# A final norm that moves into the experts' program, with the last expert's rows added by a one-hot product

## The chip, the cores and the metric

The kernel runs on one core of a Trainium2 chip. The metric is the device time of one execution in microseconds (us), smaller is better. The core has five engines that run their own instruction streams and meet at semaphores: TensorE (PE in the rows; PEld is its weight loading), VectorE (DVE), ScalarE (ACT), GpSimd (POOL) and SyncE (SP), which here only issues DMAs.

## What is computed

One encoder layer over a prompt of 512 and a sample of 1024 tokens of width 1024 (12 tiles of 128 tokens: 4 of the prompt, 8 of the sample). Attention and a state-space mixer come first; they are not touched. Then comes the mixture of experts, in which each of 16 experts chooses its tokens (64 of the prompt, 128 of the sample), and a last norm:

```python
def _ec_moe(h, w_router, w_gate, w_up, w_down):
    ...
    gate, idx = lax.top_k(aff.T, cap)
    xe = tok[idx]
    hid = jax.nn.silu(jnp.einsum('ecd,edf->ecf', xe, w_gate)) * jnp.einsum('ecd,edf->ecf', xe, w_up)
    ye = jnp.einsum('ecf,efd->ecd', hid, w_down) * gate[..., None].astype(h.dtype)
    out = jnp.zeros_like(tok).at[idx.reshape(-1)].add(ye.reshape(-1, d))
    return out.reshape(b, s, d)

    # in the layer, and after it
    return x + g2 * _ec_moe(h, w_router, w_gate, w_up, w_down)
    ...
    return _rmsnorm(x, final_norm_w)
```

All is in float32. The expert width is 2048.

## The kernel before

`encoder_layer` runs its stages one after the other. Each stage is a block of programs, one for each engine, and a barrier of all engines stands between blocks. The last two stages are `experts` and `final`.

`experts` walks through the 16 experts, and in each through 4 slabs (`fs`) of 512 hidden columns. A slab has 12 units of 128x1024 weights: for each of 4 column groups (`fc`) one of the gate (kind 0) and one of the up matrix (kind 1), then 4 of the down matrix (kind 2). A step is one `fc` of one `fs`, so an expert has 16 steps. SP loads the slabs in halves into three raw tiles (`raw[0]` and `raw[1]` lie in the tile `keys_or_w_out`, `raw[2]` is `slab_down`). ScalarE copies a unit to its high part (L2464), ten units ahead of TensorE; VectorE subtracts for its low part (L2524), eight units ahead. TensorE multiplies high and low parts (L2665, L2666), ScalarE and VectorE add the two halves up, take silu and product, and split the hidden values in two again (L2582 to L2587), and TensorE adds the down product to the banks `y_banks` (L2678, and L2642 for the prompt's low weights). TensorE begins step s only when the hidden values of step s-2 are there. The order on each engine is written out by hand in `body`. In steps 8 to 13 of every expert but the last, TensorE turns the next expert's gathered rows (`turn_x`) in spare columns of the banks, and ScalarE and VectorE drain them (`drain_x`).

When an expert is done, `weigh` on VectorE multiplies its rows by the gates and by a row of the layer's gate (L2563). The prompt's 64 rows lie in two halves of the bank, so ScalarE first copies one half (`copy_low`, L2480) and VectorE adds the other (L2560). POOL then scatters the 128 and the 64 weighted rows with an adding indirect DMA into the tensor `residual` in HBM (L2437). For all experts but the last this runs beside the next expert. For the last nothing runs beside it: POOL waits until both scatters have landed, and the block ends.

`final` is the next block. SP loads tile after tile of `residual` (L2735) into four buffers. ScalarE squares and sums (L2752) and takes the root (L2754), VectorE takes the reciprocal (L2768) and multiplies with it and the norm's weight (L2773), and POOL issues the store (L2743). The weight is first spread over the partitions by 8 small fp32 matmuls (L2001); the profile records an fp32 matmul that isn't a transpose as two. The first four tiles are the prompt's; the eight of the sample are a hardware loop of two turns. A load of a later tile waits for the product of the tile four before it.

## Time and profile before

| | us |
|---|---|
| median of three runs | 2969.93 |
| lowest and highest | 2969.90 and 2974.16 |
| the profiled execution, in all | 2971.95 |
| its span in the trace | 2970.3 |

The profile is of one execution. Times in the rows count from the start of its span. A timeline row gives start, length, engine, source line, operation, what is written and read, and in brackets the idle time ahead of it with what ended it. Rows with "x4" are merged: the length is that of all four from the first start to the last end. TensorE runs at 1.2 or 2.4 GHz; the granted clock of a stretch is 0.50 or 1.00 for these, and between them where it changed within the stretch.

### The profile page before, as it was taken

How to read it: one execution, taken by the hardware profiler on the slowest of the kernel's cores; microseconds unless marked ns; L12 is line 12 of the kernel's file. 1: busy time of each engine (PE TensorE's matmuls, PEld its weight loads, DVE VectorE, ACT ScalarE, POOL GpSimd, SP SyncE). 2: the span in 40 equal slices, each digit the busy share in tenths (PEclk: the TensorE clock that was granted, in tenths of full speed). 3: DMA queues.
4: the chain of work that ended last, by engine and by line, in shares of the span. 5: the costliest groups of instructions: out<-in, count | busy, mean ns of one | idle time of the engine just before them, and what ended most of it. 6: DMA issues, size and time to landing. Idle time of an engine off the chain costs nothing. (4 is left out here: it accounts for less than half of the span.)

```text
span 2970.3 us, 50523 instructions
## 1 busy us (share of the span) xinstructions
PE 2744.9 (92%) x17710; PEld 2391.8 (81%) x17710; DVE 2155.6 (73%) x4142; ACT 1522.5 (51%) x2876; POOL 219.5 (7%) x202
## 2 busy tenths in 40 slices
PE   5999687999988939999999999999999999999992
PEld 4999455566667738999999999999999999999992
DVE  3565776676765577878878878878878878778773
ACT  4453444444543315555555555555555555555552
POOL 0000022121110000000000000000000000000001
PEclk8999898999999969999999999999999999999996
DMA  6111310212224428678677677677677677677655
GB/s 258 67 64 58 121 39 30 96 59 95 100 89 155 155 106 275 219 243 257 221 242 254 223 239 254 220 241 254 222 241 253 222 244 250 223 247 249 223 182 181
DMA packets 359719, 547.39 MB, mean 184 GB/s; under 512 B 14785, under 2 KB 287937, under 8 KB 359617
## 3 DMA queue, kind: packets, MB, share of 16 engines
q1 hardware_dynamic: 350720, 514.59, 50.7%
q0 software_dynamic: 8896, 31.46, 4.6%
q8 instruction: 62, 1.02, 0.1%
q14 instruction: 41, 0.33, 0.0%
HBM read 493.51 MB, written 52.49 MB: 184 GB/s over the span
## 5 line engine op out<-in xcount | busy, mean ns | idle before, releaser
L2665 PE MATMUL banks<-rowsT_parts,weights_high 128*128 128x384 f32 x4096 | 1213.3, 359 | 11.6 <-DVE hidden_parts L2587 7.5
L2666 PE MATMUL banks<-rowsT_parts,weights_low 128*128 128x192 f32 x4096 | 1026.8, 251 | 0.0
L2666 PEld LDWEIGHTS banks<-rowsT_parts,weights_low 128*128 128x128 f32 x4096 | 781.8, 191 | 22.4
L2665 PEld LDWEIGHTS banks<-rowsT_parts,weights_high 128*128 128x128 f32 x4096 | 770.5, 188 | 23.3 <-DVE hidden_parts L2587 10.2
L2524 DVE TENSOR_TENSOR weights_low<-keys_or_w_out,weights_high 128x1024 fp32r<-128x1024 f32 x512 | 603.7, 1219 | 1.4 <-ACT weights_high L2464 1.4
L2464 ACT ACTIVATE weights_high<-keys_or_w_out 128x1024 fp32r<-128x1024 f32 x512 | 524.3, 1050 | 39.6 <-PEq L2262 39.6
L2574 DVE TENSOR_TENSOR h_or_keys_or_sums<-banks,h_or_keys_or_sums 128x192 f32<-128x192 f32 x512 | 181.8, 355 | 317.7 <-ACT h_or_keys_or_sums L2490 317.7
L2678 PE MATMUL banks<-weights_high,hidden_parts 128*128 128x512 f32 x1536 | 403.6, 391 | 0.0
L2490 ACT ACTIVATE h_or_keys_or_sums<-banks 128x192 f32<-128x192 f32 x512 | 165.6, 323 | 454.0 <-PE banks L2642 332.4
L2678 PEld LDWEIGHTS banks<-weights_high,hidden_parts 128*128 128x128 f32 x1536 | 283.5, 188 | 56.1
L2524 DVE TENSOR_TENSOR weights_low<-slab_down,weights_high 128x1024 fp32r<-128x1024 f32 x256 | 311.7, 1218 | 0.0
L2464 ACT ACTIVATE weights_high<-slab_down 128x1024 fp32r<-128x1024 f32 x256 | 262.6, 1051 | 0.0
L2498 ACT ACTIVATE silu_gate<-h_or_keys_or_sums 128x192 f32<-128x192 f32 x256 | 92.8, 363 | 228.0 <-DVE h_or_keys_or_sums L2574 228.0
L2642 PE MATMUL banks<-weights_low,hidden_parts 128*64 128x512 f32 x512 | 200.7, 393 | 0.0
L2437 POOL DMA_INDIRECT residual<-weighted,rows_out x32 | 49.8, 1555 | 1665.9 <-DVE weighted L2563 1665.9
L1825 PE MATMUL banks<-keys_or_w_out,arena_attend 96*128 96x512 f32 x320 | 160.8, 609 | 6.2 <-DVE arena_attend L1748 4.3
L2678 PE MATMUL banks<-weights_low,hidden_parts 128*128 128x512 f32 x512 | 157.7, 389 | 0.0
L1553 ACT ACTIVATE arena_attend<-banks 128x512 f32<-128x512 f32 (+1 forms) x96 | 50.5, 526 | 170.3 <-PE banks L1838 170.0
L2205 PE MATMUL banks<-w_out_high,mixed_parts 128*128 128x512 f32 x384 | 127.3, 399 | 2.8 <-DVE mixed_parts L2168 2.3
L1603 DVE TENSOR_REDUCE mix_top<-banks 128x1 f32<-128x1024 f32 (+1 forms) x96 | 100.2, 1043 | 25.4 <-PE banks L1825 25.4
L1838 PEld LDWEIGHTS banks<-masks,arena_attend 128*128 128x128 f32 x640 | 74.8, 141 | 53.4 <-issue 29.6
L995 PE MATMUL banks<-w_in_high,h_parts 128*128 128x512 f32 (+1 forms) x384 | 116.7, 381 | 0.0
(314 smaller groups left out, 3627.5 us busy)
## 6 DMA issues: line engine op xcount, KB each, us to landing
keys_or_w_out<-w_gate SPq DMA_DIRECT2D x128, 1024.0 KB, 5.3
keys_or_w_out<-w_up SPq DMA_DIRECT2D x128, 1024.0 KB, 6.9
slab_down<-w_down SPq DMA_DIRECT2D x128, 1024.0 KB, 4.9
arena_attend<-w_ada SPq DMA_DIRECT2D x8, 2048.0 KB, 7.6
arena_attend<-ssd_tiles SPq DMA_DIRECT2D x12, 992.0 KB, 9.1
arena_inputs<-w_ada SPq DMA_DIRECT2D x4, 2048.0 KB, 11.5
ssd_tiles<-arena_inputs SPq DMA_DIRECT2D x24, 256.0 KB, 2.0
mixed<-arena_attend SPq DMA_DIRECT2D x12, 512.0 KB, 2.9
```

Of the source, the lines that this page charges most:

```text
L995: mm = nc.tensor.matmul(out, a, b, start=(k == 0 and n == 0), stop=(k == KD - 1 and n == 2))
L1603: nc.vector.tensor_reduce(top[:, h % 2:h % 2 + 1], core.banks[:, h % 2 * 1024:h % 2 * 1024 + keys_n], AX_X, ALU.max).then_inc(topped, 1)
L1825: mm = nc.tensor.matmul(core.banks[:, h % 2 * 1024 + k0:h % 2 * 1024 + k0 + 512], qT[j][0:DQK, h, :], kT[0:DQK, h, k0:k0 + 512], start=Tru ...
L2205: mm = nc.tensor.matmul(core.ps[6 * j + half], a, b[:, k, cols], start=(k + n == 0), stop=(k == 7 and n == 2))
L2464: nc.scalar.activation(like(n, w_hi), unit_of(raw, n), ACT.Copy).then_inc(unit_hi, 1)
L2490: nc.scalar.activation(sums[:, kind, fc % 2], core.ps[2 * (fc % 2) + kind][:, CT:2 * CT], ACT.Copy).then_inc(low_out, 1)
L2524: nc.vector.tensor_tensor(like(n, w_lo), unit_of(raw, n), like(n, w_hi[:].bitcast(F32)), ALU.subtract).then_inc(unit_lo, 1)
L2574: nc.vector.tensor_tensor(sums[:, kind, fc % 2], core.ps[2 * (fc % 2) + kind][:, 0:CT], sums[:, kind, fc % 2], ALU.add).then_inc(sum_done, 1)
L2642: return nc.tensor.matmul(y_banks[1][0:CAP[0], cols], h_parts[:, fc, prompt_hi], w_lo[:, UNITS.index((2, fc)), cols], start=False, stop=en ...
L2665: nc.tensor.matmul(out[:, 0:2 * CT], w_hi[:, u, block], x[:, k, :], start=k == 0, stop=False)
L2666: mm = nc.tensor.matmul(out[:, 0:CT], w_lo[:, u, block], x[:, k, 0:CT], start=False, stop=k == KD - 1)
L2678: mm = nc.tensor.matmul(y_banks[b][:, cols], h_parts[:, fc, tokens], w[:, u, cols], start=step == 0 and first, stop=step == STEPS - 1 and ...
```

## The change

The stage `final` is gone; its work is done at the end of the block of `experts`.

- SP loads the residual's 12 tiles in three DMAs of four tiles into the three raw tiles, each when VectorE has read the last of the weights there, and once the scatters of the first 15 experts have landed. The tiles are taken in the order sample 0 to 7, prompt 0 to 3 (`tail`). The last expert's rows are not scattered.
- In steps 8 to 13 of the last expert, where the others turn and drain rows, TensorE spreads the final norm's weight and a row of numbers 0 to 127 (`tail_row`), and VectorE copies these, builds small columns (`slots`: each row's token number less the tile's first, and the prompt's gates, doubled over both halves of the partitions) and compares them into one-hot matrices, one of 128x128 for each tile (`tail_rows`). They lie in the buffers of the gathered rows, which now have 128 partitions for the prompt too.
- The prompt's rows are not added up before the weighing: all 128 partitions of the bank, both halves, are weighed at once, and the one-hot matrix has each token twice.
- TensorE multiplies for each tile the one-hot matrix with the weighted rows in fp32, two matmuls of 512 columns, in three pairs of banks in turn (`add_rows`). VectorE adds the bank to the loaded residual in place (`add_last`). ScalarE squares, sums and takes the root (`square`). VectorE takes the reciprocal, two tiles behind its additions (`normalise`), and for eight tiles multiplies by it and the weight in one operation. For tiles 1, 3, 5 and 7 (`BY_ACT`) ScalarE multiplies by the reciprocal and POOL by the weight, POOL only when VectorE's own product of the next tile is done. SP stores the tiles in order.

```diff
+            for b in range(2):
+                sp.wait_ge(y_out[b], (NE - 1) * 16)
+            for n, (r, lo) in enumerate(((1, 0), (1, 4), (0, 0))):
+                sp.wait_ge(unit_lo, (NE - 1) * (FS * NU) + (FS - 1) * NU + UNITS.index((n, 3)) + 1)
+                rows = (TILES[r][0] + lo) * P
+                sp.dma_start(raw[n][:].rearrange("p (t d) -> p t d", t=4),
+                             core.residual[rows:rows + 4 * P, :].rearrange("(t p) d -> p t d", p=P)).then_inc(tail_in[n], 16)
+            for n, g in enumerate(tail):
+                if n in BY_ACT:
+                    sp.wait_ge(out_pool, BY_ACT.index(n) + 1)
+                else:
+                    sp.wait_ge(out_dve, len([m for m in range(n + 1) if m not in BY_ACT]))
...
-            turn(NE - 1, False)
-            for b in range(2):
-                pool.wait_ge(y_out[b], NE * 16)
+            for n in BY_ACT:
+                pool.wait_ge(scaled_done, BY_ACT.index(n) + 1)
+                pool.wait_ge(out_dve, len([m for m in range(n + 2) if m not in BY_ACT]))
+                nc.gpsimd.tensor_tensor(res[n], res[n], weight, ALU.mult).then_inc(out_pool, 1)
...
-            copy_low(NE - 1)
+            nc.scalar.activation(rms[:, 0:1], core.eps[:, 0:1], ACT.Sqrt).then_inc(root, 1)
+            def square(n):
+                act.wait_ge(last_added, n + 1)
+                nc.scalar.activation(junk, res[n], ACT.Square, accum_out=ss[:, n:n + 1]).then_inc(sq_done, 1)
+                act.wait_ge(sq_done, n + 1)
...
+                nc.scalar.activation(rms[:, n:n + 1], ss[:, n:n + 1], ACT.Sqrt, bias=core.eps[:, 0:1],
+                                     scale=1.0 / D).then_inc(root, 1)
+            for n in range(NT + 1):
+                if n < NT:
+                    square(n)
+                if n - 1 in BY_ACT:
+                    act.wait_ge(rstd_done, n)
+                    nc.scalar.activation(res[n - 1], res[n - 1], ACT.Copy, scale=rstd[:, n - 1:n]).then_inc(scaled_done, 1)
...
+                else:
+                    dve.wait_ge(row_taken, 5)
+                    dve.wait_ge(slot_done, 4)
+                    for b, (n0, n1) in enumerate(((0, 8), (8, NT))):
+                        n = n1 - n0
+                        nc.vector.tensor_tensor(rows_of[b][:, 0:n * P].rearrange("p (t q) -> p t q", t=n),
+                                                iota.unsqueeze(1).broadcast_to([P, n, P]),
+                                                slots[:, n0:n1].unsqueeze(2).broadcast_to([P, n, P]),
+                                                ALU.is_equal).then_inc(hot_done, 1)
...
-            for b in range(2):
-                weigh(NE - 1, b)
+            weigh(NE - 1, 0)
+            def add_last(n):
+                dve.wait_ge(tail_in[n // 4], 16)
+                dve.wait_ge(last_mm, n + 1)
+                nc.vector.tensor_tensor(res[n], res[n], tail_bank(n), ALU.add).then_inc(last_added, 1)
+            def normalise(n):
+                dve.wait_ge(root, n + 2)
+                nc.vector.reciprocal(rstd[:, n:n + 1], rms[:, n:n + 1]).then_inc(rstd_done, 1)
+                if n not in BY_ACT:
+                    dve.wait_ge(rstd_done, n + 1)
+                    nc.vector.scalar_tensor_tensor(out=res[n], in0=res[n], scalar=rstd[:, n:n + 1], in1=weight,
+                                                   op0=ALU.mult, op1=ALU.mult).then_inc(out_dve, 1)
+            for n in range(NT + 2):
+                if n < NT:
+                    add_last(n)
+                if n == 1:
+                    nc.vector.scalar_tensor_tensor(out=weighted[1][:], in0=y_banks[1], scalar=slots[:, 13:14], in1=gain[:, 0, :],
+                                                   op0=ALU.mult, op1=ALU.mult).then_inc(y_done[1], 1)
+                if n >= 2:
+                    normalise(n - 2)
...
+            def tail_row(s):
+                if s >= 2:
+                    pe.wait_ge(row_taken, s - 1)
+                if s < 4:
+                    for kind in range(2):
+                        mm = nc.tensor.matmul(tail_spare(s, kind), core.col("final", 2 * s + kind).broadcast_to([P, P]), core.ident,
+                                              start=True, stop=True)
...
+            def add_rows(n):
+                b = int(n >= 8)
+                if n in (0, 8):
+                    pe.wait_ge(y_done[b], NE)
+                if n >= 3:
+                    pe.wait_ge(last_added, n - 2)
+                at = P * (n - 8 * b)
+                for half in range(2):
+                    mm = nc.tensor.matmul(tail_bank(n)[:, 512 * half:512 * half + 512], rows_of[b][:, at:at + P],
+                                          weighted[b][:, 512 * half:512 * half + 512], start=True, stop=True)
+                mm.then_inc(last_mm, 1)
```

What stands in a row on VectorE at the end of the experts in the kernel before, up to the first tiles of `final`:

```order
L2563 SCALAR_TENSOR_TENSOR weighted<-banks,gates,gain_rows 128x1024
L2560 TENSOR_TENSOR weighted<-banks,weighted 64x1024
L2563 SCALAR_TENSOR_TENSOR weighted<-weighted,gates,gain_rows 64x1024
L2381 UNCONDITIONAL_BRANCH
L2758 UNCONDITIONAL_BRANCH
L2763 COPY arena_final<-banks 128x512 x2
L2768 RECIPROCAL final_rstd<-final_rms 128x1
L2773 SCALAR_TENSOR_TENSOR arena_final<-arena_final,final_rstd 128x1024
```

The same place in the changed kernel. The tile `keys_or_w_out` holds eight of the residual's tiles, and `h_or_keys_or_sums` the small columns and the norm's weight:

```order
L2618 SCALAR_TENSOR_TENSOR weighted<-banks,gates,gain_rows 128x1024
L2709 TENSOR_TENSOR keys_or_w_out<-keys_or_w_out,banks 128x1024 x2
L2723 SCALAR_TENSOR_TENSOR weighted<-banks,h_or_keys_or_sums,gain_rows 128x1024
L2709 TENSOR_TENSOR keys_or_w_out<-keys_or_w_out,banks 128x1024
L2713 RECIPROCAL h_or_keys_or_sums<-h_or_keys_or_sums 128x1
L2716 SCALAR_TENSOR_TENSOR keys_or_w_out<-keys_or_w_out,h_or_keys_or_sums 128x1024
L2709 TENSOR_TENSOR keys_or_w_out<-keys_or_w_out,banks 128x1024
L2713 RECIPROCAL h_or_keys_or_sums<-h_or_keys_or_sums 128x1
L2709 TENSOR_TENSOR keys_or_w_out<-keys_or_w_out,banks 128x1024
L2713 RECIPROCAL h_or_keys_or_sums<-h_or_keys_or_sums 128x1
```

The two branches between blocks are gone; the prompt's weighing stands behind two additions, and from there each tile has an addition and a reciprocal, every second one a product too.

On VectorE in steps 12 and 13 of the last expert, the changed kernel:

```order
L2640 TENSOR_SCALAR h_or_keys_or_sums<-h_or_keys_or_sums 128x1 x12
L2670 TENSOR_TENSOR hidden<-silu_gate,h_or_keys_or_sums 128x192
L2672 CAST hidden_parts<-hidden 128x192
L2675 TENSOR_TENSOR hidden_parts<-hidden,hidden_parts 128x128
L2675 TENSOR_TENSOR hidden_parts<-hidden,hidden_parts 128x64
L2579 TENSOR_TENSOR weights_low<-slab_down,weights_high 128x1024
L2660 TENSOR_TENSOR h_or_keys_or_sums<-banks,h_or_keys_or_sums 128x192
L2579 TENSOR_TENSOR weights_low<-slab_down,weights_high 128x1024
L2660 TENSOR_TENSOR h_or_keys_or_sums<-banks,h_or_keys_or_sums 128x192
L2647 TENSOR_TENSOR rows<-h_or_keys_or_sums 128x1024
L2647 TENSOR_TENSOR rows<-h_or_keys_or_sums 128x512
L2670 TENSOR_TENSOR hidden<-silu_gate,h_or_keys_or_sums 128x192
```

The tiny operations (L2640, and the copies ahead of them) and the two comparisons (L2647) stand ahead of the hidden values of their step; without them the rows are those of the kernel before.

On TensorE, the end of the kernel before and then of the changed one:

```order
L2678 MATMUL banks<-weights_high,hidden_parts 128x512 x2
L2642 MATMUL banks<-weights_low,hidden_parts 64x512 x2
L2381 UNCONDITIONAL_BRANCH
L2779 UNCONDITIONAL_BRANCH
L2001 MATMUL banks<-masks,cols 128x128 x8
```

```order
L2814 MATMUL banks<-weights_high,hidden_parts 128x512 x2
L2776 MATMUL banks<-weights_low,hidden_parts 64x512 x2
L2768 MATMUL banks<-weighted,rows 128x512 x24
L2403 UNCONDITIONAL_BRANCH
```

The 24 one-hot matmuls (L2768) follow the last down product directly; the small ones for the weight have moved into steps 8 to 12.

## Rows read from the trace of the kernel before

**Rows 1.** The page's head: span, then busy time and share of each engine
```profile
span 2970.3 us, 50523 instructions
PE 2744.9 (92%) x17710; PEld 2391.8 (81%) x17710; DVE 2155.6 (73%) x4142; ACT 1522.5 (51%) x2876; POOL 219.5 (7%) x202
```
**Rows 2.** Timeline from 2913 us, all engines: start, length, engine, line, operation, idle before
```profile
2913.01 0.62 PE L2642 MATMUL banks<-weights_low,hidden_parts 128*64 128x512 f32 x2
...
2913.78 1.28 DVE L2563 SCALAR_TENSOR_TENSOR weighted<-banks,gates,gain_rows 128x1024 f32<-128x1024 f32 x1 [7.38 <-issue]
2914.98 1.21 DVE L2560 TENSOR_TENSOR weighted<-banks,weighted 64x1024 f32<-64x1024 f32 x1
2915.85 1.58 POOL L2437 DMA_INDIRECT residual<-weighted,rows_out  x1 [92.04 <-DVE weighted L2563]
...
2918.41 1.44 POOL L2437 DMA_INDIRECT residual<-weighted,rows_out  x1 [0.98 <-DVE weighted L2563]
...
2929.35 3.75 PE L2001 MATMUL banks<-masks,cols 128*128 128x128 f32 x16 [15.72 <-PEq L2381]
```
**Rows 3.** The same timeline in the final stage, ScalarE and VectorE
```profile
2935.38 1.04 ACT L2752 ACTIVATE arena_final<-arena_final 128x1024 f32<-128x1024 f32 x1
...
2936.75 1.04 ACT L2752 ACTIVATE arena_final<-arena_final 128x1024 f32<-128x1024 f32 x1
2937.22 0.16 DVE L2768 RECIPROCAL final_rstd<-final_rms 128x1 f32<-128x1 f32 x1 [0.15 <-DVE arena_final L2773]
...
2938.86 0.16 DVE L2768 RECIPROCAL final_rstd<-final_rms 128x1 f32<-128x1 f32 x1 [0.15 <-DVE arena_final L2773]
```
**Rows 4.** Stretches: length, TensorE busy, granted clock, DMA share, GB/s moved
```profile
2916.00:2917.00 1.00, 0.00 (x0) 0.69 0.00 0
2917.00:2918.00 1.00, 0.00 (x0) 0.50 0.00 0
2932.00:2933.00 1.00, 1.00 (x6) 0.50 1.03 414
...
876.00:887.00 11.00, 7.59 (x124) 1.00 0.57 204
```
**Rows 5.** TensorE's fp32 records: two timeline rows, two by line (ns min/median/max)
```profile
704.61 1.09 PE L1838 MATMUL banks<-masks,arena_attend 128*128 128x128 f32 x8
...
364.42 1.95 PE L1825 MATMUL banks<-keys_or_w_out,arena_attend 96*128 96x512 f32 x4 [1.03 <-DVE arena_attend L1598]
...
L1825 PE MATMUL banks<-keys_or_w_out,arena_attend x320: 590/592/1062, 364.4 to 873.1; 96*128 96x512 f32 x160
...
L2001 PEld LDWEIGHTS banks<-masks,cols x16: 288/333/338, 2929.3 to 2932.5; 128*128 128x128 f32 x16
```
**Rows 6.** VectorE's timeline in the last expert's steps 12 and 13, and tiny operations
```profile
2891.63 0.36 DVE L2582 TENSOR_TENSOR hidden<-silu_gate,h_or_keys_or_sums 128x192 f32<-128x192 f32 x1
...
2896.18 0.36 DVE L2582 TENSOR_TENSOR hidden<-silu_gate,h_or_keys_or_sums 128x192 f32<-128x192 f32 x1
...
2897.21 1.22 DVE L2524 TENSOR_TENSOR weights_low<-slab_down,weights_high 128x1024 fp32r<-128x1024 f32 x1
...
346.17 0.17 DVE L1216 TENSOR_TENSOR arena_attend<-h_or_keys_or_sums,rope 128x16 f32<-128x16 f32 x1
346.26 0.17 DVE L1217 TENSOR_TENSOR arena_attend<-h_or_keys_or_sums,rope 128x16 f32<-128x16 f32 x1
```
**Rows 7.** DMA issues of the whole run: size of each, median us from issue to landing
```profile
residual<-arena_output SPq DMA_DIRECT2D x12, 512.0 KB, 2.6
...
ssd_tiles<-arena_inputs SPq DMA_DIRECT2D x1, 896.0 KB, 4.3
...
residual<-weighted,rows_out POOLq DMA_INDIRECT x32, 6.2
...
ssd_tiles<-arena_inputs SPq DMA_DIRECT2D x12, 32.0 KB, 1.5
```
**Rows 8.** POOL's products of 128x1024 by line, ns min/median/max
```profile
L1430 POOL TENSOR_TENSOR arena_attend<-masks,arena_attend x22: 1896/1897/1978, 388.0 to 830.9; 128x1024 f32<-128x1024 f32 x22
```

More of the change, by code:

```diff
@@ L2433, in scatter @@
                     ins.then_inc(rows_copied, 1)
[L2434 removed]
+                pool.wait_ge(rows_copied, e * 4 + 6)
                 for b in range(2):
@@ L2578, in body @@
                             drain_x(e + 1, step - TURN0)
+                        if not after and 0 <= step - TURN0 < TURNS:
+                            tail_rows(step - TURN0)
                         dve.wait_ge(sil_done, e * STEPS + (step + 1))
@@ L2654, in unit @@
                     turn_x(e + 1, step - TURN0)
+                if kind == 0 and not after and 0 <= step - TURN0 < 5:
+                    tail_row(step - TURN0)
                 if kind == 2:
@@ L2787 @@
+            pe.wait_ge(hot_done, 2)
+            for n in range(NT):
+                add_rows(n)
 SHARED = 8192
```

132 lines of the change are left out of this document (54 added, 78 removed).

## The prediction

> **What bounds the kernel now.** I read the page's head, then the timeline of the last 60 us, then the clock by stretches, and went back for prices. TensorE works for 92% of the span [rows 1]; all of that but the end is the same program before and after, so only the last expert and what follows it can move. The reader is to see this there: TensorE's last matmul of the experts ends at 2913.63 (2913.01 + 0.62). VectorE weighs the sample rows until 2915.06, then adds and weighs the prompt's, and POOL issues the two scatters at 2915.85 and 2918.41 [rows 2]. Then no compute engine does anything until 2929.35, when the final stage starts: a scatter takes a median 6.2 us to land [rows 7], and the rest of the 9.5 us after POOL's issue ended (2919.85) is the change of program block. From 2929.38 to 2970.3 the final stage runs, 40.9 us for 12 tiles, fed by loads of the residual. So 56.7 us of the span [rows 1] lie behind TensorE's last matmul, in which the matrix engine does 3.75 us of work.
>
> **What goes.** The scatter of the last expert, its landing, the block change and the reload of 12 tiles leave the path: 2929.35 - 2913.63 = 15.7 us of the 56.7, and the loads of the 40.9. The three loads of four tiles each now wait only for the last use of each slab; VectorE's last subtraction from the down slab starts at 2897.21 [rows 6], 15 us ahead of TensorE's end when it is done, and 2 MB at the 414 GB/s of [rows 4] take 5 us. They are hidden; if not, the first addition would wait. ScalarE's table load for Sqrt moves to where ScalarE idles before the tail: zero.
>
> **What is added in front of TensorE's end.** (a) Nine fp32 matmuls of 128 columns, two records each. Eight records of that form take 1.09 us, so about 0.116 us a record at full clock [rows 5]: 18 x 0.116 = 2.1 us on TensorE, which is always busy there; at the half clock's 3.75 us for 16 records [rows 2] it would be 4.2. I take 2.1, since the clock is full in this stage. (b) On VectorE two copies a step (steps 8 to 11) where the other experts drain the turned rows, covered as those are. Step 12 gets a copy and 17 tiny operations: a pair of independent 128x16 additions starts 0.09 us apart [rows 6], so 0.3 + 17 x 0.1 = 2.0 us. Step 13 gets the one-hot comparison of 1024 and 512 columns, 1.2 + 0.7 = 1.9 us by the 1.22 us of a 1024-column operation [rows 6]. Queued behind them are the hidden products and the splits. Products of step 12 begin at 2891.63 and of step 13 at 2896.18, with subtractions of 1.22 us between [rows 6]. Pushed by 2.0 us the first end at 2894.6; split, sum, split and sum put the second comparison at 2897.5, so step 13's products end at 2900.5 instead of 2897.3. TensorE wants them for step 15, near 2900. I take a stall of 0.5 us; bounds 0 and 2.0 (if tiny operations cost 0.16 us each, as one RECIPROCAL does [rows 3]). TensorE thus ends at E = 2913.6 + 2.1 + 0.5 = 2916.2.
>
> **The tail, counted from E.** VectorE weighs the sample rows until E+1.43 (0.15 + 1.28 [rows 2]). TensorE then adds two fp32 matmuls of 512 columns a tile, four records: a run of four takes 1.95 us, the last record 0.59, so 0.45 a record and 1.8 a tile [rows 5] (those have 96 rows instead of 128; columns set the time). First tile ready at E+3.4, second at E+5.2. VectorE's addition of 1024 columns from PSUM costs 1.21 [rows 2], 1.25 with its handoff: E+4.7, E+6.5; then the prompt weighing, 1.3: E+7.8. From here TensorE is ahead (1.8 a tile, three bank pairs) and VectorE is the bound. One reciprocal with one product takes 1.64 from one reciprocal to the next (2937.22 to 2938.86 [rows 3]); a reciprocal alone 0.31. Ten more additions 12.5, eight products with reciprocals 8 x 1.64 = 13.1, four reciprocals alone 1.2: E+34.7. ScalarE's square and root repeat every 1.37 us (2935.38 to 2936.75 [rows 3]) and its scaling copy costs 1.05, 3.8 us for two tiles; VectorE needs 4.45 for the same two, so ScalarE follows.
>
> POOL multiplies tiles 1, 3, 5 and 7, 1.90 us each [rows 8], each starting when VectorE's next own product is done. The last begins at E+28.5 and ends at E+30.4. Stores are issued in tile order by SP, so tiles 7 and 8 go out then, 9, 10 and 11 later. Five tiles are 2.62 MB; at the 414 GB/s seen in the final stage [rows 4] 6.3 us, plus 1.5 us for the fixed part, the whole of a 32 KB store [rows 7]: E+38.3. The last store alone would give 34.8 + 2.6 [rows 7] = E+37.4. A store of 896 KB takes 4.3 us against 1.5 for 32 KB [rows 7], about 310 GB/s between them: 8.4 us, E+40.4. I take 38.3, the stretch with many transfers queued being nearer to this tail, and 1.0 us from landing to the end of the span. Sum: 2916.2 + 38.3 + 1.0 = **2955.5**, 14.8 less than the profiled span of 2970.3. That execution took 2971.95 in all, 2.0 above the median of 2969.93; the gain is taken from the median: **2955.1, about 2955 us**.
>
> **What the tail rests on.** TensorE's clock. After TensorE stopped at 2913.63 it fell to half only between 2916 and 2917 (0.69 in that stretch, 0.50 in the next [rows 4]). The new pause lasts only 1.4 us. In the tail TensorE is busy 1.8 of each 2.2 us, at the end 1.8 of 2.9; in 876:887 it was busy for 7.59 of 11.00 us and the granted clock was 1.00 [rows 4]. So I take the full clock.
>
> Of 22 POOL products of this size in this trace none took less than 1896 ns or more than 1978 [rows 8], so whatever VectorE did beside them cost POOL no more than 0.08 us each; what it cost VectorE the rows don't tell. The Trainium skill (SBUF — State Buffer, "Who interferes with whom") says that a VectorE instruction with two SBUF inputs and a POOL instruction that reads SBUF exclude one another whole, and that one with a PSUM input does not take part. By that rule the additions run free beside POOL's products, and only the product of tile 9, ready 0.35 us before POOL ends tile 7, would wait: the sum would be 2955.9 span instead of 2955.5. No row here shows the exclusion. The same skill (DMA: Bandwidth & Descriptors, "Where 436 GB/s comes from") lets HBM bind at some 358 GB/s per core; the 414 GB/s of [rows 4] is above it, though it counts both directions. By the page the five last stores take an estimated 7.3 us, and the sum would be 1.0 higher.
>
> **Rivals.** (1) Stores don't overlap: each of 512 KB takes its whole 2.6 us [rows 7]. Tile 1 leaves POOL at E+17.1, eleven stores follow it: E+45.7, with the end 2962.9, or 2962.5 on the median. Against it: the 896 KB store, which moves 512 KB more than another for far less than 2.6 us more. (2) The clock falls to half and stays. A record is then 0.9 and a tile 3.6 us: 12 tiles from E+1.5 are 43.2, then 1.25, 1.8 for square, root and reciprocal, 1.3, 2.6 and 1.0: E+52.7 = 2968.9, or 2968.5, no change. For it: TensorE does pause and its busy share falls to 60% in the last tiles. If it falls only at the start or the end, 2958 to 2961. (3) Handoffs cost more than I count: each tile crosses four engines, and 0.4 us more per tile gives 2960. (4) Slower: the weight loads of the one-hot matmuls aren't hidden at half clock. A load takes 333 ns there [rows 5], a record 0.9 + 0.33 = 1.23, a tile 4.9: 59 us, and with the 8 us of its end E+68.5 = 2984.7, 14 slower. It decides from (2976.2 - 2916.2 - 9.5) / 12 = 4.2 us a tile. Against it: 16 records with 16 loads took 3.75 us at half clock [rows 2], less than one record and one load apart. (5) The step-13 comparison stalls TensorE by more than 2 us: 2957 to 2958; inside the range.
>
> **How the numbers follow.** What a measurement of this kernel can tell from no change is about 0.2%, 5.9 us: faster means below 2964.0, slower above 2975.9. Forecast (2950 to 2958) 0.62; partly half clock 0.10; costlier handoffs 0.12; stores one by one 0.06; half clock throughout 0.06; slower 0.04. The likeliest is 2955. The lower end takes no stall (-0.5), the last store alone (-0.9) and nothing between landing and end (-1.0), and 2 us for additions that start before the operation ahead of them ends, as rows at 2914.98 do: 2950. The upper end takes in (1) and (3): 2964. All but the last two cases are faster, with a little of them lost over 2964: faster 0.87, same 0.09, slower 0.04.
>
> **What the profile of the changed kernel would show.** Right: no idle stretch between TensorE's last expert matmul and the one-hot ones beyond 1.5 us; one-hot records 0.45 us apart with the clock at 1.0; VectorE nearly without waits from the third tile; its last product some 35 us after the experts' last matmul; stores of the last tiles bunched behind POOL's. TensorE's experts would end 2 to 3 us later than 2913.6. Wrong: additions that wait for TensorE at 3.6 us a tile (rival 2), output stores with a steady 2.6 us apart and VectorE long done (rival 1), VectorE's reciprocals waiting for ScalarE's roots (rival 3), a hole on TensorE before step 15 (rival 5). The 15.7 us of the block change can't come back unless the residual's loads are late, which would show as the first addition waiting for a DMA.

## The result, and the profile after

The changed kernel takes 2953.83 us (median of five runs, 2953.09 to 2955.82) against 2970.50 for the kernel before (five runs, 2969.90 to 2974.16): 0.9941 of its time, with a 95% interval of 0.9927 to 0.9956. That is 16.7 us faster. The forecast was 2955 in a range of 2950 to 2964.

The profiled execution has a span of 2954.0 us, its head against [rows 1]:

```profile
span 2954.0 us, 50539 instructions
PE 2767.3 (94%) x17760; PEld 2400.7 (81%) x17760; DVE 2164.8 (73%) x4175; ACT 1523.9 (52%) x2880; POOL 218.4 (7%) x190
```

The timeline around TensorE's last matmul of the experts, all engines, stands against [rows 2]. Its columns are the same: start, length, engine, line, operation, idle time before.

```profile
2916.29 0.62 PE L2776 MATMUL banks<-weights_low,hidden_parts 128*64 128x512 f32 x2
2917.06 1.28 DVE L2618 SCALAR_TENSOR_TENSOR weighted<-banks,gates,gain_rows 128x1024 f32<-128x1024 f32 x1 [7.38 <-issue]
2918.49 7.96 PE L2768 MATMUL banks<-weighted,rows 128*128 128x512 f32 x18 [1.58 <-DVE weighted L2618]
2920.56 1.22 DVE L2709 TENSOR_TENSOR keys_or_w_out<-keys_or_w_out,banks 128x1024 f32<-128x1024 f32 x1 [2.21 <-PE banks L2768]
...
2922.27 1.22 DVE L2709 TENSOR_TENSOR keys_or_w_out<-keys_or_w_out,banks 128x1024 f32<-128x1024 f32 x1 [0.49 <-PE banks L2768]
```

The experts' last matmul ends at E = 2916.29 + 0.62 = 2916.91. Where TensorE stood idle for 15.72 us before it spread the weight [rows 2], it now waits 1.58 us for the sample's weighing and goes on with the one-hot products. VectorE waits for TensorE only twice, 2.21 and 0.49 us, ahead of the first two additions.

From 2938 us on, VectorE, POOL and SyncE, in rows of that timeline:

```profile
2938.27 1.22 DVE L2709 TENSOR_TENSOR slab_down<-slab_down,banks 128x1024 f32<-128x1024 f32 x1
2938.50 2.37 POOL L2491 TENSOR_TENSOR keys_or_w_out<-keys_or_w_out,h_or_keys_or_sums 128x1024 f32<-128x1024 f32 x1 [1.34 <-DVE keys_or_w_out L2716]
2939.40 0.16 DVE L2713 RECIPROCAL h_or_keys_or_sums<-h_or_keys_or_sums 128x1 f32<-128x1 f32 x1
2939.48 1.20 DVE L2709 TENSOR_TENSOR slab_down<-slab_down,banks 128x1024 f32<-128x1024 f32 x1
2940.59 0.16 DVE L2713 RECIPROCAL h_or_keys_or_sums<-h_or_keys_or_sums 128x1 f32<-128x1 f32 x1
2940.79 1.28 DVE L2716 SCALAR_TENSOR_TENSOR slab_down<-slab_down,h_or_keys_or_sums 128x1024 f32<-128x1024 f32 x1
2941.99 1.21 DVE L2709 TENSOR_TENSOR slab_down<-slab_down,banks 128x1024 f32<-128x1024 f32 x1
2942.22 2.36 POOL L2491 TENSOR_TENSOR keys_or_w_out<-keys_or_w_out,h_or_keys_or_sums 128x1024 f32<-128x1024 f32 x1 [1.35 <-DVE slab_down L2716]
2943.12 0.15 DVE L2713 RECIPROCAL h_or_keys_or_sums<-h_or_keys_or_sums 128x1 f32<-128x1 f32 x1
2943.31 2.34 DVE L2716 SCALAR_TENSOR_TENSOR slab_down<-slab_down,h_or_keys_or_sums 128x1024 f32<-128x1024 f32 x1
2944.98 3.82 SPq L2450 DMA_DIRECT2D y_prompt<-slab_down  x4
...
2947.16 1.28 DVE L2716 SCALAR_TENSOR_TENSOR slab_down<-slab_down,h_or_keys_or_sums 128x1024 f32<-128x1024 f32 x1
```

Three things are to be seen. VectorE has no bracket at all: from its third addition on it is never idle. An addition takes 1.13 us from its start to that of the reciprocal behind it (2938.27 to 2939.40), and a reciprocal with a product 1.40 (2940.59 to 2941.99). POOL's product takes 2.36 us, and the one VectorE product that begins well before POOL's end, tile 9's at 2943.31, takes 2.34 us instead of 1.28 (tile 8's, at 2940.79, begins 0.08 us before POOL's end and keeps 1.28). VectorE's last product ends at 2948.44, which is E+31.5, and POOL's at 2944.58, E+27.7.

The stretches of the end: length, TensorE's busy time, its granted clock, DMA share, GB/s. They stand against [rows 4].

```profile
2917.00:2918.00 1.00, 0.00 (x0) 1.00 0.00 0
2918.00:2919.00 1.00, 0.51 (x2) 1.00 0.00 0
...
2939.00:2942.00 3.00, 0.53 (x2) 0.93 0.63 257
...
2944.00:2945.00 1.00, 0.00 (x0) 0.50 0.21 82
2945.00:2946.00 1.00, 0.00 (x0) 0.50 0.61 250
2946.00:2947.00 1.00, 0.00 (x0) 0.50 1.01 414
2947.00:2948.00 1.00, 0.00 (x0) 0.50 1.03 422
2948.00:2949.00 1.00, 0.00 (x0) 0.50 1.02 418
2949.00:2950.00 1.00, 0.00 (x0) 0.50 1.02 418
2950.00:2951.00 1.00, 0.00 (x0) 0.50 1.04 426
2951.00:2952.00 1.00, 0.00 (x0) 0.50 0.67 274
```

The clock is at 2.4 GHz through the pause of 1.58 us and through all one-hot products, and falls to 1.2 GHz only when these are over. The stores move 414 to 426 GB/s and the last bytes land near 2951.65, with 2.35 us from there to the end of the span.

The time from E to the end of the span, called the tail below, went from 56.67 us (2970.3 - 2913.63) to 37.09. E itself is 3.3 us later here, but it scatters: in ten profiled executions of kernels with this same code ahead of E (this one and nine experiments, without the first one and the one with a longer step 13) it lay between 2911.1 and 2920.0, on average at 2915.6. So the experiments are compared by their tails, each from one profiled execution, and by medians only where several us separate them.

### The profile page after: what moved, and what is told of

Same layout as the page of the kernel before. It is cut to its first block, busy times and chain, and to the rows that moved or that the text cites. A ratio compares the mean times of both kernels' runs of the same rounds, so it can differ in the third digit from the quotient of the medians.

```text
span 2954.0 us, 50539 instructions
## 1 busy us (share of the span) xinstructions
PE 2767.3 (94%) x17760; PEld 2400.7 (81%) x17760; DVE 2164.8 (73%) x4175; ACT 1523.9 (52%) x2880; POOL 218.4 (7%) x190
## 3 DMA queue, kind: packets, MB, share of 16 engines
q8 instruction: 62, 1.02, 0.1%
## 4 chain that ended last, share of the span: by engine, by line
PE 54%; DVE 4%; issue 3%; ACT 1%; DVEq 0%; ACTq 0%
PE banks L2801 23%; PE banks L2814 15%; PE banks L2802 10%; PE banks L2776 4%; DVE weights_low L2579 1%; PE banks L2743 1%; DVE h_or_keys_or_sums L2660 1%; DVE weighted L2615 1%; DVE hidden L2670 0%; ACT h_or_keys_or_sums L2529 0%; DVE hidden_parts L2672 0%; DVE hidden_parts L2675 0%; PE banks L2001 0%; DVE keys_or_w_out L2709 0%; DVE slab_down L2716 0%
## 5 line engine op out<-in xcount | busy, mean ns | idle before, releaser
L1748 DVE COPY arena_attend<-banks 128x512 f32<-128x512 f32 (+1 forms) x96 | 57.5, 599 | 82.9 <-PE banks L1838 82.9
```

## The experiments

Eleven kernels were made and run, each from the changed kernel. Where no median is given, the kernel ran once. The tails of the changed kernel, of the longer step 13 and of the left-out matmuls, whose order on VectorE is the same, agree within 0.1 us (37.09, 37.10 and 37.10) although their E lie 11 us apart, so differences of some tenths can be read. A tile is counted as in the tail: 0 to 7 are the sample's, 8 to 11 the prompt's.

**Keeping the scatter, without the block change.**

```diff
-                sp.wait_ge(y_out[b], (NE - 1) * 16)
+                sp.wait_ge(y_out[b], NE * 16)
...
-                sp.dma_start(raw[n][:].rearrange("p (t d) -> p t d", t=4),
-                             core.residual[rows:rows + 4 * P, :].rearrange("(t p) d -> p t d", p=P)).then_inc(tail_in[n], 16)
+                for t in range(4):
+                    sp.dma_start(res[4 * n + t], core.residual[rows + P * t:rows + P * t + P, :]).then_inc(tail_in[4 * n + t], 16)
...
+            scatter(NE - 1)
...
+            copy_low(NE - 1)
...
-            weigh(NE - 1, 0)
+            for b in range(2):
+                weigh(NE - 1, b)
...
-                if n < NT:
-                    add_last(n)
...
-            for n in range(NT):
-                add_rows(n)
```

> The changed kernel with the last expert's rows scattered and the 12 tiles reloaded one by one behind that, as in the kernel before, but inside the experts' block; no one-hot products and no additions. It splits the 15.7 us before the final stage into the scatter's landing and the block change. From the end of TensorE's last expert matmul to the end of the span the kernel before takes 56.7 us and the changed one 37.1. Theory: the scatter and the reload are most of it, and the block change some 4 to 5 us: about 48 to 52 us here, span near 2967. Rival 1: the block change was nearly the whole of the gain: 38 to 42 us. Rival 2: the block change cost nothing, the gain is the one-hot product's: 55 to 57 us, the time of the kernel before.

The median was 2961.88 us (ratio 0.9970, 0.9958 to 0.9983), with E at 2914.04 and a tail of 45.66 us. From its timeline, the second scatter and the first reload (SPq is SyncE's queue):

```profile
2918.82 1.44 POOL L2476 DMA_INDIRECT residual<-weighted,rows_out  x1 [0.98 <-DVE weighted L2620]
2923.66 4.27 SPq L2442 DMA_DIRECT2D keys_or_w_out<-residual  x8
2926.86 1.06 ACT L2562 ACTIVATE gain_rows<-keys_or_w_out 128x1024 f32<-128x1024 f32 x1 [10.19 <-DMA keys_or_w_out<-residual]
```

The scatters are as in [rows 2], but the first reload goes out 9.6 us after E (2923.66 - 2914.04) instead of 15.75 (2929.38 - 2913.63). The scatter still lands before it, so the 6.1 us between them are the price of the block change alone. The other 9.6 us are the scatter's: weighing, issue and landing. From the first reload to the end it takes 36.0 us here against 40.9 in the kernel before, and the stretches say what fills them: the DMA engines are at their limit (mean DMA share 1.00 and 1.02, 397 and 410 GB/s). In the kernel before the share was 0.76 from 2932 to 2941 us and reached this level only after it. Whether its four buffers, its table load or the spreading of the weight made that start slower was not separated.

```profile
2930.00:2940.00 10.00, 0.00 (x0) 0.00 (x0) 3.40 (x8) 9.10 (x18) 4.36 (x2) 0.50 1.00 397
2940.00:2950.00 10.00, 0.00 (x0) 0.00 (x0) 6.98 (x9) 8.51 (x17) 5.01 (x3) 0.50 1.02 410
```

In these rows the five busy times are TensorE, its weight loading, VectorE, ScalarE and POOL. So the tail came out below the 48 to 52 us that were expected, and above the rival's 38 to 42: the block change is only a part of the gain, but no small one, and the reload runs closer to what the DMA engines allow than in the kernel before. At this rate it can't fall far below that: 12 tiles read and written are 12.6 MB, some 31 us at 400 GB/s, whatever the engines do. So the 19.6 us of the tail are 6.1 for the block change, 4.9 for the faster reload and 8.6 for the rest. These last 8.6 us, from 45.7 to 37.1, come with the one-hot product: it lets the reads go ahead of E, so that the tail has only the writes.

**POOL doesn't wait for VectorE's next product.**

```diff
                 pool.wait_ge(scaled_done, BY_ACT.index(n) + 1)
-                pool.wait_ge(out_dve, len([m for m in range(n + 2) if m not in BY_ACT]))
```

> POOL multiplies as soon as ScalarE has scaled, without waiting for VectorE's own product of the next tile. In the changed kernel VectorE's product of tile 9 took 2.34 us instead of 1.28 while POOL was at tile 7. Theory (a VectorE operation with two SBUF inputs and a POOL product that reads SBUF exclude one another): three or four of VectorE's or POOL's products are stretched by 0.5 to 2.4 us each, VectorE ends 2 to 5 us later, tail 39 to 42 us against 37.1. Rival (the 2.34 us had another cause): no stretched product but tile 9's, POOL earlier, tail 36 to 37.

The median was 2960.69 us (0.9962, 0.9948 to 0.9976), the tail 43.59, 6.5 us longer than with the wait. Two of the four places in its timeline:

```profile
2932.74 3.48 DVE L2715 SCALAR_TENSOR_TENSOR keys_or_w_out<-keys_or_w_out,h_or_keys_or_sums 128x1024 f32<-128x1024 f32 x1
2932.78 2.35 POOL L2490 TENSOR_TENSOR keys_or_w_out<-keys_or_w_out,h_or_keys_or_sums 128x1024 f32<-128x1024 f32 x1 [109.80 <-ACT keys_or_w_out L2571]
...
2938.64 3.47 DVE L2715 SCALAR_TENSOR_TENSOR keys_or_w_out<-keys_or_w_out,h_or_keys_or_sums 128x1024 f32<-128x1024 f32 x1
2938.68 2.36 POOL L2490 TENSOR_TENSOR keys_or_w_out<-keys_or_w_out,h_or_keys_or_sums 128x1024 f32<-128x1024 f32 x1 [3.55 <-ACT keys_or_w_out L2571]
```

Each VectorE product that meets a POOL product takes 3.47 us: POOL's whole 2.36 and then its own 1.1. POOL's length doesn't change (2.34 to 2.38 in every run that multiplies by the norm's weight). So VectorE waits until POOL's product has ended, and then takes its own time. Other overlaps say the same: the length of the product is the overlap plus 1.07 to 1.09 us, with 1.41 for an overlap of 0.34 and 2.45 for 1.36 (both in the first experiment), 2.34 for 1.27 in the changed kernel, 3.48 for 2.39 here. In all of these VectorE is the one that pays, but no run has a POOL product that begins well inside a VectorE product, so who would pay then isn't shown. It happened four times, 4 x 2.2 = 8.8 us against 1.06 in the changed kernel: VectorE's end moves by 7.7, from E+31.5 to E+39.2. Each stretch lies within the expected 0.5 to 2.4 us, but with four of them VectorE ends 7.7 us later and not 2 to 5, and the tail is 43.6 and not 39 to 42; the rival, no other stretched product and a tail of 36 to 37, is out.

**All products on VectorE.**

```diff
-BY_ACT = (1, 3, 5, 7)
+BY_ACT = ()
```

> VectorE makes all twelve products, POOL and ScalarE none. Theory (VectorE's chain sets the end): four more products of 1.36 us less the 1.06 us of the stretched one, VectorE ends 4.4 us later, and the last store lands sooner because none is queued ahead: tail 40 to 41 us against 37.1. Rival (the last stores, queued behind POOL's tile 7, set the end): tail within 1 us of 37.1, since the stores are spread.

The median was 2958.31 us (0.9951, 0.9934 to 0.9967), the tail 39.88; VectorE ends at E+35.8, 4.3 later, and no product is stretched. A reciprocal with a product costs 1.40 in VectorE's row and one alone 0.08 (2939.40 to 2939.48): four products more are 5.3, less the 1.06 of the stretch 4.2. POOL's help is worth 2.8 us of the tail with the wait, and without it costs 3.7 more than no help at all.

**A pause ahead of the one-hot products.** Four subtractions whose results nobody reads, 4.63 us, stand on VectorE ahead of the sample's weighing.

```diff
+            dve.wait_ge(unit_used, NE * (FS * NU))
+            for i in range(4):
+                nc.vector.tensor_tensor(w_lo[:, i, :], w_hi[:, 0, :].bitcast(F32), w_hi[:, 1, :].bitcast(F32), ALU.subtract)
             weigh(NE - 1, 0)
```

> VectorE makes four useless subtractions of 128x1024 (1.13 us each, 4.5 in all) between TensorE's last expert matmul and the weighing, so that TensorE pauses 6 us instead of 1.6. Theory (the tail rests on the clock staying up through the short pause): the granted clock is 0.5 when the one-hot products begin, the first tile takes about 3.4 us instead of 1.7, and the tail is 37.1 + 4.5 + 2 to 4 = 43.5 to 46 us. Rival (TensorE is far enough ahead for the clock not to matter): 41.6 us.

```profile
2921.30 8.22 PE L2771 MATMUL banks<-weighted,rows 128*128 128x512 f32 x13 [6.01 <-DVE weighted L2618]
2925.17 1.22 DVE L2712 TENSOR_TENSOR keys_or_w_out<-keys_or_w_out,banks 128x1024 f32<-128x1024 f32 x1 [4.01 <-PE banks L2771]
2927.49 1.22 DVE L2712 TENSOR_TENSOR keys_or_w_out<-keys_or_w_out,banks 128x1024 f32<-128x1024 f32 x1 [1.10 <-PE banks L2771]
```

TensorE now pauses for 6.01 us instead of 1.58. The granted clock is 0.50 from 2921 to 2925, 0.71 in the next two us and 1.00 from 2927. The first addition waits 4.01 us for its tile instead of 2.21, the second 1.10 instead of 0.49. The tail is 44.01 us, 6.9 more for a pause that is 4.4 longer: half clock costs 2.5 us, and only in the first two tiles, since the clock comes back under the products. The first tile takes 3.87 us from its first matmul to its addition; less the 0.35 of the handoff, this is 0.88 for each of four records, and the weight loads lie within it. So the rival with exposed loads (1.23 a record) has no ground even at half clock.

**Each one-hot matmul twice.**

```diff
-                for half in range(2):
+                for half in (0, 1, 0, 1):
```

> Every one-hot matmul is made twice, so that a tile costs TensorE 3.42 us instead of 1.71: the price that the half clock would have had in the tail. Nothing else changes. Theory (TensorE has slack in the tail, but less than half): TensorE becomes the bound, 12 x 3.42 = 41.0 from E+1.6 to E+42.6, then an addition 1.2, square and root 1.8, reciprocal and product 1.3, store 3.1 and 2.3 to the span's end: a tail of about 52 us after TensorE's last expert matmul (E), against 37.1. Rival (VectorE's queue would still be the bound with all the pauses filled): under 42. The granted clock should stay at 1.00 through the tail.

The profiled run has a tail of 54.3 us. All 96 records stand in one row without a pause, at full clock, and VectorE waits for them:

```profile
2920.58 41.44 PE L2768 MATMUL banks<-weighted,rows 128*128 128x512 f32 x96 [1.58 <-DVE weighted L2618]
```

This is the size of the prediction's rival 2, half clock throughout: with a tile at 3.45 us (41.44 / 12) the tail is back near the 56.7 us of the kernel before, and the one run took 2975.0 us in all. It is 2 us more than expected, since three products, not one, stand behind the last addition in VectorE's order (its last ends 5.6 us after TensorE). 

**Ten of the 24 one-hot matmuls left out.** The second 512 columns of tiles 2 to 11 aren't multiplied.

```diff
-                for half in range(2):
+                for half in range(2 if n < 2 else 1):
```

> From the third tile on only the first half's one-hot matmul is made (the second 512 columns of these ten tiles are left out, so they are added from whatever the bank holds). TensorE's part of a tile falls from 1.71 to 0.86 us. Theory (VectorE's queue bounds the tail from the third tile, TensorE does not): VectorE's last product ends at E+31.5 as before, within 0.3, and the tail stays at 37.1, within 0.4. Rival (TensorE or its handoff still adds to each tile): VectorE ends earlier, by up to 10 x 0.2 = 2 us. The clock falls to half earlier, which changes nothing.

The tail is 37.1 us and VectorE's last product ends at E+31.5, both as before to 0.1 us. TensorE makes 28 records in the tail instead of 48 and nothing moves: from the third tile on VectorE's own queue is the bound.

**A longer step 13.** The two comparisons of step 13 are made three times.

```diff
-                    for b, (n0, n1) in enumerate(((0, 8), (8, NT))):
+                    for turn, b, (n0, n1) in [(t, b, c) for t in range(3) for b, c in enumerate(((0, 8), (8, NT)))]:
...
+                        if b == 0 and turn:
+                            dve.wait_ge(hot_done, 2 * turn)
...
-            pe.wait_ge(hot_done, 2)
+            pe.wait_ge(hot_done, 6)
```

> The two comparisons of step 13 are made three times over, 3.6 us more on VectorE in front of the hidden values. Theory (the prediction's stall was absent because some 1 us of slack was left): the hidden values of step 13 come at about 2906.4 where TensorE wants them near 2904, so TensorE pauses 2 to 3 us ahead of step 15, and the time from VectorE's last sum of step 12 (2894.39 in the changed kernel) to E is 24.5 to 25.5 instead of 22.5. Rival (TensorE is further ahead of its need and doesn't look at these values so early): 22.5 to 23.0. Tail after E unchanged at about 37 us.

What TensorE waited for (us in total, times, longest), and its stretches in this kernel:

```profile
PE banks L2803 <- DVE hidden_parts L2677: 3.6, 1, 3.6
...
2904.00:2905.00 1.00, 0.00 (x0) 1.00 0.00 0
...
2906.00:2907.00 1.00, 0.00 (x0) 1.00 0.00 0
2907.00:2908.00 1.00, 0.48 (x3) 1.00 0.00 0
2908.00:2909.00 1.00, 1.00 (x8) 0.76 0.06 16
2909.00:2910.00 1.00, 1.00 (x6) 0.50 0.75 61
```

TensorE stood still for 3.6 us by its waits, for the hidden values of step 13, and then ran some 3 us at half clock. From VectorE's last sum of step 12 to E it took 27.85 us instead of 22.52: 5.3 us for 3.7 us of work on VectorE, since the half clock adds 1.7 to the pause. The tail is the same, 37.1. The stall is thus real, only the changed kernel didn't reach it: 3.73 us of delay gave 3.6 us of pause, so it had about 0.1 us to spare. I had expected 1 us of slack, and a pause of 2 to 3 us.

**Three products on POOL.**

```diff
-BY_ACT = (1, 3, 5, 7)
+BY_ACT = (1, 3, 5)
```

> Tile 7's product goes from POOL to VectorE, so POOL makes tiles 1, 3 and 5 only. VectorE's queue gets 1.2 us longer: its last product ends at E+32.7 instead of E+31.5, but the stores of tiles 7 and 8 leave earlier, since POOL holds them back no longer. Theory A (the end is set by five stores queued behind POOL's last product, at 420 GB/s): the tail is no longer than 37.1 and the last bytes land within 0.5 us of E+34.7, or earlier. Theory B (the last product of VectorE sets the end): the tail grows by 1.2 us, to 38.3.

The median was 2952.42 us (0.9940, 0.9926 to 0.9954), not to be told from the changed kernel. VectorE's last product ends 1.3 us later, at E+32.9, and the tail grows only by 0.3, to 37.4. The last bytes land 2.1 us behind VectorE's end, where it was 3.2. Neither theory holds alone: some 1 us of the tail is a backlog of stores, the rest is VectorE.

**Two additions beside POOL's last product.**

```diff
+                if n == 10:
+                    normalise(8)
                 if n < NT:
                     add_last(n)
...
-                if n >= 2:
+                if n >= 2 and n != 10:
```

> VectorE makes tile 8's product before the addition of tile 10 instead of after it, so that two additions and no product of VectorE lie beside POOL's last product (tile 7), and POOL starts it one addition earlier. Theory (a VectorE operation with two SBUF inputs waits out a POOL product, one with a PSUM input does not): no VectorE product over 1.4 us, its last one ends at E+30.5 instead of E+31.5, POOL's last at E+26.6 instead of E+27.7, the tail 36.0 instead of 37.1. Rival (the stretched product of 2.34 us came from something else, such as the stores' reads): it stays, and the tail stays at 37.

The median was 2956.47 us (0.9939, 0.9925 to 0.9953), the tail 37.04, unchanged. The timeline of the place:

```profile
2939.25 2.36 POOL L2491 TENSOR_TENSOR keys_or_w_out<-keys_or_w_out,h_or_keys_or_sums 128x1024 f32<-128x1024 f32 x1 [1.34 <-DVE keys_or_w_out L2716]
...
2940.66 0.17 DVE L2713 RECIPROCAL h_or_keys_or_sums<-h_or_keys_or_sums 128x1 f32<-128x1 f32 x1 [0.35 <-ACT h_or_keys_or_sums L2564]
2940.86 1.83 DVE L2716 SCALAR_TENSOR_TENSOR slab_down<-slab_down,h_or_keys_or_sums 128x1024 f32<-128x1024 f32 x1
2942.61 2.34 DVE L2709 TENSOR_TENSOR slab_down<-slab_down,banks 128x1024 f32<-128x1024 f32 x2
```

The two additions (x2, one row) take 2.34 us together, 1.17 each, beside POOL's product from 2942.84 to 2945.19: an operation with one input from PSUM doesn't wait. In this the theory held. But tile 8's product, drawn forward, now meets the end of POOL's tile 5 (2941.61) and takes 1.83, and its reciprocal waits 0.35 for ScalarE's root. 0.55 + 0.35 is nearly the 1.06 that was to be gained: the collision was moved, not removed.

**POOL multiplies by spread numbers.** POOL's second operand is eight numbers, each spread over 128 columns, so that the norm's weight is left out for tiles 1, 3, 5 and 7.

```diff
-                nc.gpsimd.tensor_tensor(res[n], res[n], weight, ALU.mult).then_inc(out_pool, 1)
+                nc.gpsimd.tensor_tensor(res[n].rearrange("p (a b) -> p a b", a=8), res[n].rearrange("p (a b) -> p a b", a=8),
+                                        weight[:, 0:8].unsqueeze(2).broadcast_to([P, 8, 128]), ALU.mult).then_inc(out_pool, 1)
```

> POOL multiplies by eight numbers spread over 128 columns each instead of by the norm's weight, so that only one of its two operands is a full stream of 1024 (this leaves the right weights out of tiles 1, 3, 5 and 7). Theory (POOL's product takes 2.37 us instead of the 1.90 of the rows of before because both operands are full streams, where those had two spread ones): 1.90 us here, or a value between if each operand counts by itself (about 2.1). Rival (the traffic beside it in the tail makes it slow): 2.37. By the exclusion theory VectorE's product of tile 9 shrinks with it, from 2.34 to 1.8 to 2.1 us, VectorE's end moves from E+31.5 to 31.0 to 31.3 and the tail loses 0.2 to 0.8 us.

The line's group in the trace (ns, min/median/max):

```profile
L2491 POOL TENSOR_TENSOR keys_or_w_out<-keys_or_w_out,h_or_keys_or_sums x4: 1893/1898/1902, 2925.3 to 2936.4; 128x1024 f32<-128x1024 f32 x4
```

One spread operand gives the 1.90 us of [rows 8], in the same place beside the same traffic. VectorE's product of tile 9 shrinks with it to 1.88, VectorE ends at E+31.1 and the tail is 36.67.

**Stores in the order of readiness.**

```diff
-            for n, g in enumerate(tail):
+            for n in (0, 2, 1, 4, 3, 6, 5, 8, 7, 9, 10, 11):
+                g = tail[n]
```

> SyncE issues the stores in the order in which the products come ready (tile 2 before 1, 4 before 3, 6 before 5, 8 before 7) instead of in tile order; no compute engine changes. In the changed kernel the last bytes land 2.85 us after the last store's issue, with four stores queued ahead of it; with three POOL products, where VectorE's last product ended 1.3 us later, it was 1.8 us and the tail grew by only 0.3. Theory (a backlog of stores behind POOL's tile 7 costs about 1 us): VectorE's last product still at E+31.5, the last bytes at about E+33.7, the tail 36.0 to 36.3. Rival (the last store has the same path length whatever is queued): the tail stays at 37.0 to 37.2.

The median was 2950.70 us (0.9940, 0.9926 to 0.9953), VectorE's end at E+31.5 as before, the tail 36.01. The rates before the end (length, granted clock, DMA share, GB/s):

```profile
2944.00:2945.00 1.00, 0.50 1.02 418
2945.00:2946.00 1.00, 0.50 0.89 365
2946.00:2947.00 1.00, 0.50 0.56 225
```

The last bytes land near 2946.6, E+33.7, and 2.1 us behind VectorE's end instead of 3.2. So the backlog is confirmed: in tile order, tile 8, long ready, waits for POOL's tile 7, and five stores of 1.25 us each then stand behind E+27.7. But 1 us cannot be told by medians of kernels whose E scatters by some us; it is shown by the tails. No experiment beats the changed kernel by a measurable amount; this one is the best by its tail.

## Why the prediction was right, and which of its terms were not

The time lies 1.2 us under the forecast of 2955, and the sign and the mechanism were right. But the sum is better than its terms, and that is in part luck. In the forecast of the tail VectorE's order was 3.2 us and the stores 0.7 us too long, POOL's product 0.5 us and the end of the span 1.3 us too short; in all the tail came 2.2 us shorter. And 1.6 us of scatter between executions, which no term describes, made up for part of this. Without it the profiled gain is 56.7 - 37.1 - 1.7 = 17.9 us, where 14.8 were forecast.

**TensorE's end, forecast E = 2916.2, measured 2916.9.** Of the 3.3 us by which E is later, 1.6 were there before the last expert's step 8, where no work had been added: that is the scatter between executions. 1.7 came in between step 8 and step 15, against 2.1 for the records and 0.5 for a stall. (The 0.116 us a record behind the 2.1 is a distance between starts; 1.09 / 8 of [rows 5] holds the last record's whole length too.) The tiny operations of step 12 took 1.47 us, from 2894.66 to 2896.13, where 2.0 were forecast, the two comparisons 1.81 of 1.9, and no stall came. The bounds of that stall, 0 and 2.0, were well put: the longer step 13 showed that it was missed by 0.1 us. What the bounds didn't hold is that a stall can also take the clock along: the one of 3.6 us did, for 1.7 us more, and whether one of 2.0 would isn't shown.

**Block change and scatter.** That 15.7 us go and no hidden load comes late was right: the first addition waited for TensorE alone. A load of 2 MB took a median 9.8 us from issue to landing (the last 8.8) and not 5, but the last was issued at 2903.95, 13 us ahead of E. The split was wrong, which the sum didn't need: the forecast had some 3 us for the block change, the rest of the 9.5 us behind POOL's last issue after 6.2 for a landing. The first experiment has 3.4 us from the end of that issue to the reload (2920.26 to 2923.66), so 6.1 are the block change, 9.6 are the scatter with its weighing and issue, and of the 40.9 us behind them a large part was the traffic of the reload itself.

**VectorE's order, forecast E+34.7, measured E+31.5.** This is the term with the largest error. An addition is 1.13 us apart from what follows it and not 1.25 (ten of them, 1.2 us in all), a reciprocal alone 0.08 and not 0.31 (four, 0.9), and a reciprocal with its product 1.40 and not 1.64 (eight, 1.9). The 1.64 of [rows 3] was read as work, but its rows have an idle time of 0.15 ahead of the reciprocal; in the changed kernel an operation starts some 0.08 us before the one ahead of it ends, unless it needs its result. That is 4.0 us too much. The forecast had put 2 us for this into its lower bound, as the rows at 2914.98 suggested, and not into the sum. Against it stands the stretched product of tile 9, 1.06 us, which the sum had at zero. Together they are 3.0 of the 3.2 us.

**POOL's products, forecast 1.90 us each, measured 2.37.** The step that failed is the one from [rows 8]: those 22 products have the same shape, but both of their operands are spread: one block of 128 columns read eight times, and eight numbers. With one spread operand the tail's product took 1.90 too. The Trainium skill (GPSIMD Engine Reference, "3.1 Elementwise — side-by-side cycle accounting") has 4497 ns for an addition of 2048 fp32 numbers a partition and puts it to two inputs that share one read port. Half of that is an estimated 2.25 us, which the 2.37 of this trace is near to, 5% above; what a spread operand saves the page doesn't say.

**The exclusion.** The product of tile 9 begins 1.27 us before POOL ends tile 7 (2943.31 and 2944.58) and takes 2.34, which is 1.27 and its own 1.1. Without POOL's wait four such products took 3.47 each, and two additions that read PSUM took 1.17 each beside POOL. The Trainium skill (SBUF — State Buffer, "Who interferes with whom") has VectorE and POOL share a pair of ports as an exclusive lock, for which a VectorE instruction with two SBUF inputs contends with a POOL instruction that reads SBUF. The trace agrees in all three; how long this form waits is shown by these rows. The forecast's sum by that page was 0.35 us, against 1.06 measured, since POOL's product was taken to be 0.47 us shorter and VectorE's order ran faster than forecast.

**Stores, forecast E+38.3 for the last landing and 1.0 to the end, measured E+34.7 and 2.35.** From POOL's last end to the last bytes it took 7.1 us (2944.58 to 2951.65), against 7.8 in the sum (6.3 and 1.5); the rates of 414 to 426 GB/s are those assumed, so the 6.3 held and the fixed part was 0.8. That five stores queue behind POOL's last product was right, and the order of the stores shows what it costs: 1.1 us. What follows the last bytes was 1.3 us longer than forecast. All in all the tail is 37.1 us instead of 39.3: POOL's end 2.7 earlier, the stores 0.7 shorter, the end 1.3 longer. The Trainium skill (DMA: Bandwidth & Descriptors, "Where 436 GB/s comes from") has the HBM side bind at some 358 GB/s for one core. By these rows it doesn't: here are stores alone, with no read beside them, at 414 to 426 GB/s, and the measurement decides.

**The clock.** Full through the pause and the products, as forecast (rival 2 out), and half only from 2942 on, where TensorE has no more to do. The pause made longer shows what the forecast's case of a clock at half in part is worth: 2.5 us, where 2958 to 2961 had meant 3 to 6. The weight loads (rival 4) are hidden at half clock too, and at 3.45 us a tile nearly all of the gain would be gone, as rival 2 had it. Stores one by one (rival 1) are out by the rates above, costlier handoffs (rival 3) by VectorE's row without idle times.

**What stays open.** Why E scatters by up to 9 us between executions with the same code wasn't looked into; nearly all of it arises before the last expert. Nor was it tried to take the 1.7 us of spreading out of TensorE's last expert.

## What to carry to other kernels

When a tail is fed by reads, writes and several engines, find out first what it moves: the largest part of this gain isn't the block change (6.1 of 19.6 us) but that the scatter's landing and 6.3 MB of reads no longer lie behind the last matmul. The price is 1.7 us in TensorE's last expert and the wait for the first two one-hot tiles (2.21 and 0.49 us on VectorE); the other ten cost the path nothing. Once a tail is one engine's queue, price that queue by start-to-start distances where the engine is never idle, not by distances that contain a wait. And before a POOL operation is priced from another, see that its operands are of the same kind, and put it beside VectorE operations with an input from PSUM, which these runs never saw wait.

## What the hardware did that was not expected

- POOL's 128x1024 fp32 product takes 2.36 us with two full operands and 1.90 with one of them spread from eight numbers.
- VectorE's product with two SBUF inputs waits until POOL's has ended and then takes 1.1 us more: 3.47 us where both began together, even though its row starts 0.04 us before POOL's, and 1.41 for an overlap of 0.34.
- Half clock followed a pause of 3.6 or 6.0 us of TensorE and not one of 1.6. After the one of 3.6 it set in only when TensorE had begun again (1.00 in 2907 to 2908, 0.76 in 2908 to 2909), and it cost 1.7 us there and 2.5 us after the longer one.
- One change of program block costs 6.1 us with a scatter in front of it and a reload behind it.
- Independent VectorE operations start 0.08 us before the one ahead has ended, so that a 128x1 reciprocal between two additions costs 0.08 us.
